# A final norm and the mixer behind it: the transposes taken from the unscaled X, with the reciprocal roots on a diagonal

## The reference, cut to what matters

```python
def rmsnorm(x, w):                       # first block's end: "final", gain final_norm
    return x * lax.rsqrt(jnp.mean(x * x, axis=-1, keepdims=True) + EPS) * w

x = first_block(...)                     # ... ffn, then rmsnorm(x, final_norm)
hn = _rms_norm(h, e_norm_mix[i])         # second block, layer 0: h = x
p = hn @ e_w_in[i]                       # input projection of the RWKV mixer
h = h + concat(ya, yb) @ e_w_out[i]      # the residual path needs the normed x itself
```

## Time and profile before

| | us |
|---|---|
| median of 3 runs | 1972.7 (1971.6 to 1972.93) |
| the profiled execution, whole | 1973.36 |
| its span in the profile | 1971.6 |
| PE busy in the span | 1919.0 (97%) |
| DVE busy | 1522.7 (77%) |
| ACT busy | 1149.5 (58%) |
| POOL busy | 374.2 (19%) |

### The profile page before, as it was taken

One profiled execution on the slowest core, in us unless ns is written; L12 is line 12 of the kernel. 1 busy time (PEld: TensorE's weight loads), 2 busy tenths in 40 slices (PEclk: granted clock), 3 DMA queues, 4 the chain that ended last, 5 costly groups with the idle time before them and its releaser, 6 DMA issues.

```text
span 1971.6 us, 33634 instructions
## 1 busy us (share of the span) xinstructions
PE 1919.0 (97%) x12652; PEld 1684.8 (85%) x12652; DVE 1522.7 (77%) x2142; ACT 1149.5 (58%) x1717; POOL 374.2 (19%) x181
## 2 busy tenths in 40 slices
PE   7999998999999999999999899999999999999998
PEld 6888997988888889988879888888997788888886
DVE  6777886777777778777767867777787699898987
ACT  5444565544454454654455555444566677777776
POOL 2222021322222220122222232322001100000000
PEclk9999999999999999999999999999999999999999
DMA  8655441555555554255553205655553599999995
GB/s 347 201 187 187 152 160 48 200 192 191 192 176 190 191 178 172 100 206 192 187 190 130 97 3 183 202 190 188 189 196 132 199 325 354 326 356 328 356 337 207
DMA packets 73689, 401.06 MB, mean 203 GB/s; under 512 B 8288, under 2 KB 8416, under 8 KB 41440
## 3 DMA queue, kind: packets, MB, share of 16 engines
q1 hardware_dynamic: 72992, 397.55, 58.1%
q10 hardware_dynamic: 576, 1.84, 0.3%
HBM read 398.30 MB, written 1.05 MB: 203 GB/s over the span
## 4 chain that ended last, share of the span: by engine, by line
PE 88%; DVE 6%; PEld 3%; ACT 2%; issue 1%; DMA 0%; SPq 0%; ACTq 0%; DVEq 0%; PEldq 0%
PE psum L823 20%; PE psum L345 14%; PE psum L346 14%; PE psum L347 14%; PE psum L803 11%; PE psum L578 2%; PE psum L590 2%; PE psum L580 2%; PE psum L1188 1%; PE psum L3753 1%; DVE w_lo L313 1%; PE psum L359 1%; PE psum L3766 1%; PE psum L436 1%; PEld psum L347 1%
## 5 line engine op out<-in xcount | busy, mean ns | idle before, releaser
L313 DVE TENSOR_TENSOR w_lo<-ring,w_hi 128x1024 fp32r<-128x1024 f32 x498 | 741.9, 1519 | 172.4 <-ACT w_hi L306 171.6
L306 ACT ACTIVATE w_hi<-ring 128x1024 fp32r<-128x1024 f32 x744 | 738.9, 1051 | 204.6 <-PEq L539 104.6
L319 POOL TENSOR_TENSOR w_lo<-ring,w_hi 128x1024 fp32r<-128x1024 f32 x132 | 325.5, 2466 | 1093.4 <-ACT w_hi L306 1093.4
L823 PE MATMUL psum<-fT,w_hi 128*128 128x512 f32 x1760 | 422.3, 391 | 3.8 <-ACT w_hi L306 3.8
L823 PEld LDWEIGHTS psum<-fT,w_hi 128*128 128x128 f32 x1760 | 330.5, 189 | 72.2 <-ACT w_hi L306 4.2
L803 PEld LDWEIGHTS psum<-fT,w_lo 128*128 128x128 f32 x1760 | 226.0, 191 | 8.9
L345 PE MATMUL psum<-w_hi,act_hi 128*128 128x512 f32 x594 | 232.9, 392 | 0.2 <-DVE act_lo L4091 0.2
L346 PE MATMUL psum<-w_lo,act_hi 128*128 128x512 f32 x594 | 232.5, 391 | 0.0
L347 PE MATMUL psum<-w_hi,act_lo 128*128 128x512 f32 x594 | 231.1, 389 | 0.0
L803 PE MATMUL psum<-fT,w_lo 128*128 128x256 f32 x1760 | 228.7, 283 | 0.0
L888 ACT ACTIVATE up_sums<-psum 128x512 f32<-128x512 f32 x110 | 65.7, 597 | 234.5 <-PE psum L803 234.5
(11 more groups left out here) (611 smaller groups left out, 2923.4 us busy)
## 6 DMA issues: line engine op xcount, KB each, us to landing
ring<-in_stream SPq DMA_DIRECT2D x249, 1024.0 KB, 5.6
ring<-in_stream SPq DMA_DIRECT2D x248, 512.0 KB, 4.3
tables<-in_tables SPq DMA_DIRECT2D x1, 2005.0 KB, 19.6
gain_row<-in_gains ACTq DMA_DIRECT2D x3, 512.0 KB, 5.2
rows<-in_rows SPq DMA_DIRECT2D x1, 1288.0 KB, 22.4
X<-in_x SPq DMA_DIRECT2D x1, 1024.0 KB, 4.9
columns<-in_columns SPq DMA_DIRECT2D x1, 993.0 KB, 15.4
result<-X SPq DMA_DIRECT2D x3, 256.0 KB, 2.9
```

The source lines that it names most:

```text
L306: act.activation(part(w_hi, g, i), ring[:, k, i * PART:(i + 1) * PART], ACT.Copy) \
L313: dve.tensor_tensor(part(w_lo, g, i), ring[:, k, i * PART:(i + 1) * PART], part(w_hi, g, i).bitcast(F32), ALU.subtract) \
L319: pool.tensor_tensor(part(w_lo, g, 2), ring[:, k, 2 * PART:STEP], part(w_hi, g, 2).bitcast(F32), ALU.subtract) \
L823: pe.matmul(psum[:, 4 + 2 * (s % 2) + o, :], w[0][:, o, k, :], fT[:, k, :, :].rearrange("p a c -> p (a c)"), start=k == 0, stop=False, ski ...
```

## The change

At the border between the final norm and the RWKV mixer the order is turned around. Let r0 be the reciprocal roots of the final norm.

- ACT squares X in halves of 512 features, each as soon as DVE has added it; the root of a token tile takes the second half's sum, with the first half's sum plus EPS as its bias. Sums, and the product of the two gains, lie in the still unused `rstd_row`.
- DVE makes the reciprocal roots and a diagonal matrix of them for each token tile.
- PE makes the transposes as ordinary products: a chunk of the unscaled X is the stationary operand, the diagonal the moving one, which gives the transposed and scaled chunk. Nine fillers stand ahead, not 16.
- ACT and DVE take the high and low halves with the product of both gains.
- X itself is scaled on DVE behind its low halves, by the same instruction as before.
- The splits of the second step's first two parts by ACT move from the FFN's end: one behind the roots, one behind the high halves.
- `final_gain` is a new part of the column table (eight numbers a partition), which moves what is allocated behind it by 32 bytes; `m_partial` of the last layer takes the place of an existing small tile.

```diff
@@ class Places
-                 (... ("conv3", 3 * 4)])
+                 (... ("conv3", 3 * 4), ("final_gain", KT)])
@@ network_kernel
+        half_squares = rstd_row[:, 0:2 * TT].rearrange("p (h t) -> p h t", h=2)
+        first_squares, both_gains = rstd_row[:, 2 * TT:3 * TT], rstd_row[:, 4 * TT:4 * TT + KT]
@@ head_scalar, head_vector: gain_of(n) becomes head_gain(n)
+        def head_gain(n):
+            return both_gains if from_final(n) else gain_of(n)
@@ ffn_scalar
-            split_hi(act, g0 + n + 1, g0 + n + 1, (0, 1))
+            if NETWORK[at + 1][0] != "final":
+                split_hi(act, g0 + n + 1, g0 + n + 1, (0, 1))
@@ new
+        def final_head_tensor(pe, n):
+            keep_warm(pe, psum[:, 7, :], 9)
+            for t, pairs in ((0, (0, 1)), (1, (0,)), (0, (2,)), (1, (1,)), (0, (3,)), (1, (2, 3))):
+                pe.wait_ge(*after(f"final {n} diag {t}"))
+                for p in pairs:
+                    for i in range(2):
+                        k = 2 * p + i
+                        ins = pe.matmul(head_bank(n, p)[:, (i * TT + t) * P:(i * TT + t + 1) * P], X[:, t, k * P:(k + 1) * P], rstd_diag[:, t, :],
+                                        start=True, stop=True, skip_group_check=True)
+                    if t == TT - 1:
+                        ins.then_inc(*norm.tensor(f"norm {n} turn {p}"))
+
+        def final_head_scalar(act, n):
+            load_gain_row(act, NETWORK[n - 1][1])
+            act.activation(warm[:, :], eps, ACT.Sqrt)
+
+            def square(h, t):
+                c = slice(h * 512, (h + 1) * 512)
+                act.wait_ge(*after(f"x {n - 1} {t} {4 * h}"))
+                act.activation(up_sums[:, h, :, :].rearrange("p o c -> p (o c)") if t == 0 else O[:, 1, c], X[:, t, c], ACT.Square, scale=D_MODEL ** -0.5,
+                               accum_out=half_squares[:, h, t:t + 1]).then_inc(*norm.scalar(f"final {n} square {h} {t}"))
+
+            def root(t):
+                act.wait_ge(*after(f"final {n} square 1 {t}"))
+                act.wait_ge(*after(f"final {n} first"))
+                act.activation(rms[:, t:t + 1], half_squares[:, 1, t:t + 1], ACT.Sqrt, bias=first_squares[:, t:t + 1]) \
+                   .then_inc(*norm.scalar(f"final {n} root {t}"))
+
+            square(0, 0)
+            square(0, 1)
+            square(1, 0)
+            root(0)
+            square(1, 1)
+            root(1)
+            g = first_step[n] + 1
+            split_hi(act, g, g, (0,))
+            head_scalar(act, n)
+            split_hi(act, g, g, (1,))
+
+        def final_head_vector(dve, n):
+            dve.wait_ge(*after(f"final {n} square 0 1"))
+            dve.tensor_tensor(first_squares[:, :], half_squares[:, 0, :], eps.to_broadcast([P, TT]), ALU.add).then_inc(*norm.vector(f"final {n} first"))
+            dve.tensor_tensor(both_gains[:, :], col("final_gain"), gain_of(n), ALU.mult).then_inc(*norm.vector())
+            for t in range(TT):
+                dve.wait_ge(*after(f"final {n} root {t}"))
+                dve.reciprocal(rstd[:, t:t + 1], rms[:, t:t + 1]).then_inc(*norm.vector())
+                dve.wait_ge(*norm.vector.so_far())
+                dve.tensor_scalar(rstd_diag[:, t, :], ident, rstd[:, t:t + 1], None, ALU.mult).then_inc(*norm.vector(f"final {n} diag {t}"))
+            head_vector(dve, n)
+            for t, ins in enumerate(gained(dve, n - 1, X)):
+                ins.then_inc(*norm.vector(f"x {n} {t}"))
@@ the last layer's tile
-            m_partial = take("m_partial", [P, TT])
+            m_partial = rstd_f
@@ the tensor program (scalar and vector programs likewise, and "final" itself only continues)
-                    keep_warm(pe, psum[:, 7, :], 16)
-                    head_tensor(pe, at)
+                    final_head_tensor(pe, at)
```

More of the change, by code:

```diff
@@ L74 @@
                  ("r_k", 4), ("sgu_b", 4), ("sgu_w", 4 * P), ("router", KT * EXPERTS), ("lora", 512), ("g2", 512),
-                 ("cmp_k2", 2 * 64), ("cmp_v2", 2 * 64), ("pos_k", 16), ("pos_v", 16), ("conv3", 3 * 4)])
+                 ("cmp_k2", 2 * 64), ("cmp_v2", 2 * 64), ("pos_k", 16), ("pos_v", 16), ("conv3", 3 * 4), ("final_gain", KT)])
 ROW = Places([("gdn_norm", P), ("diff_norm", P), ("ln_g", 512), ("ln_b", 512),
@@ L422, in operand, with from_final @@
             return (fT_hi, fT_lo) if NETWORK[n][0] == "ffn" else (hT_hi, hT_lo)
+        def from_final(n):
+            return n > 0 and NETWORK[n - 1][0] == "final"
+        def head_gain(n):
+            return both_gains if from_final(n) else gain_of(n)
         def head_bank(n, p):
@@ L443, in head_scalar @@
                     k = 2 * p + i
-                    act.activation(operand(n)[0][:, k, :], head_bank(n, p)[:, i * SEQ:(i + 1) * SEQ], ACT.Copy, scale=gain_of(n)[:, k:k + 1]) \
+                    act.activation(operand(n)[0][:, k, :], head_bank(n, p)[:, i * SEQ:(i + 1) * SEQ], ACT.Copy, scale=head_gain(n)[:, k:k + 1]) \
                        .then_inc(*norm.scalar(f"norm {n} hi {p}"))
@@ L452, in head_vector @@
                     k = 2 * p + i
-                    dve.scalar_tensor_tensor(lo[:, k, :], head_bank(n, p)[:, i * SEQ:(i + 1) * SEQ], gain_of(n)[:, k:k + 1], hi[:, k, :].bitcast(F32),
+                    dve.scalar_tensor_tensor(lo[:, k, :], head_bank(n, p)[:, i * SEQ:(i + 1) * SEQ], head_gain(n)[:, k:k + 1], hi[:, k, :].bitcast(F32),
                                              ALU.mult, ALU.subtract).then_inc(*norm.vector(f"norm {n} hT {k}"))
@@ L4196, in _ @@
                 if kind == "final":
[L4197 to L4201, removed]
+                    continue
+                if kind != "moe":
+                    if from_final(at):
+                        final_head_scalar(act, at)
+                    else:
+                        head_scalar(act, at, (3,) if after_mixer(at) else PAIRS)
                     if at == 0:
@@ L4219, in _ @@
                 if kind == "final":
-                    if NETWORK[at - 1][0] != "moe":
-                        final_vector(dve, at)
                     continue
                 if kind != "moe":
-                    head_vector(dve, at, (3,) if after_mixer(at) else PAIRS)
+                    if from_final(at):
+                        final_head_vector(dve, at)
+                    else:
+                        head_vector(dve, at, (3,) if after_mixer(at) else PAIRS)
                     if at == 0:
@@ L4397, in pack_columns @@
     c[:, COLUMN["gain"]] = np.concatenate([per(a[n].reshape(-1)) for n in names], axis=1)
+    c[:, COLUMN["final_gain"]] = per(a["final_norm"])
     c[:, COLUMN["conv"]] = np.concatenate([per(a["l0_conv_w"][j]) for j in range(4)], axis=1)
```

## The result

| | us |
|---|---|
| median, kernel before (22 runs beside these) | 1974.73 (1969.92 to 1978.52) |
| median, changed kernel (22 runs) | 1977.78 (1975.3 to 1985.46) |
| ratio | 1.002, 95% interval 1.0013 to 1.0026 |
| the profiled execution of the changed kernel, whole | 1981.05 |
| its span (before: 1971.6) | 1979.2 |

The forecast was 1969.2, and faster by 3.5; the kernel is slower by 0.2%, 3 us by the medians and some 4 by the ratio. (The forecast counted from a median of 3 runs, 1972.7. The 22 runs beside those of the changed kernel have 1974.73, from which the same 3.5 would give 1971.2.) One row of the table already says where to look: the change takes 7 fillers out (7 x 0.226 = 1.6) and gives products of 3.88 for transposes of 3.29, which is 1 us less work, and yet PE is busy 10 us longer. So most of the time isn't in a wait.

What follows compares the result with a forecast made beforehand. PE was taken as the bound (88% of the span), so only its waits at the border could be won: the last low half from 1041.6 to 1038.1 saves 3.5, all else zero; 1972.7 - 3.5 = 1969.2, range 1967.9 to 1971.0.

Steps and rivals of the forecast that it cites:

- The border's terms: Border of final norm and RWKV: the steps from ACT's table load to the last low half at about 1038.1, saving 3.5.
- The sum of the first halves: DVE adds EPS to the first halves' sum at the border: 0.16 taken; with 0.95 all that follows is 0.8 later.
- the rival of four times a transpose: At the border each product with a 32-bit diagonal takes 0.43, 16 of them 6.9; time 1971.2, chance 0.04.
- the first rival: At the border the product costs four times a transpose: last turn 1038.9, T 1040.1, time 1971.2; chance 0.04.
- T: End of the last low half at the border: 1041.60 before, forecast about 1038.1.
- the second: The clock falls at the border all the same: 16 products take 7.2, T 1040.8, time 1971.9; chance 0.03.
- What moved behind the head: DVE's scaling of X and work behind the last low halves come later but stay hidden, with cover 0.8 and 0.6.
- The rival that made this the bound: PE waits for row product or third part behind the border: 0.5 to 1.5 lost, time 1969.9 to 1970.9; chance 0.07.
- slower than before: PE's holes in RWKV fall to half clock, at most 1.7 each; three cost 5.1, time 1974.3; chance 0.02.
- more than I count: Last layer's half-clock stretch of 6.8 shortens, up to 1.7; products 0.4 more; time 1967.5 to 1968.7; chance 0.30.

## Why the prediction was wrong, and where it was right

**The step that failed** is the one that reads "Nothing lies outside the border but the 32-byte move of the tiles behind the column table. No row shows its cost; I take zero, with half a microsecond to either side". It costs 5.6 us of PE's time by the lags, 5.9 by the starts; by the ratios of the changed kernel and of the one with the distance restored, 1.002 and 0.9986, it is 6.7 with an uncertainty of some 2.5, and by the comparison at one clock below it is 6.0 with 0.9. It acts on every product that reads hT, and so in four mixers. The half microsecond was no bound at all: no row had been put under it. The only bound that the rows could give was the number of products times a change of pitch, and in the kernel before the starts of otherwise equal products lie 113 ns apart in some runs of them and 117 to 118 in others. With those 5 ns for every one of the 2090, the bound would have been 10 us to the slow side, and the range would have held the result.

**The border's terms** held, each read from line 951's start, with the forecast's own distance from 1028.17 behind it: table load -0.72 (-0.73), first square 0.79 (0.79), root 0 at 2.96 (2.98), first product 3.83 (3.86), first high half 5.51 (5.53), first low half 6.38 (6.43), projection 7.47 (7.48), last low half 9.82 (9.93). The sum of the first halves, with bounds 0.16 and 0.95, took 0.15: the value taken from the nearer row was right, and the 0.95 was that of an instruction beside POOL's; no run here puts the same instruction with and without POOL side by side. The product with a 32-bit diagonal took two records at full clock: the eight of the first diagonal in the whole-tile version last 1.16, and 32 with all waits 3.88; so the rival of four times a transpose falls (16 x 0.43 would be 6.9). That a transpose takes half as long as such a product at full clock, an estimate in the prediction, is borne out: in the kernel with the move alone the clock fell only at 1039.8, and the transposes start 0.11 apart until then and 0.21 apart behind it, against 0.226 for a product.

Two slips in the rivals' sums changed nothing. Five falls of the clock at 1.7 would give 1977.7, not 1977. And the first rival puts T 1.2 behind its last turn, the second 1.6, with products of nearly the same length.

**What moved behind the head** stayed under cover. The diagonal of the next norm was ready at 1046.40 + 0.48 = 1046.88, 5.87 behind the last low half (6.0 forecast), and PE wanted it at 1047.99. POOL's low half ended 8.92 behind it (9.1 forecast):

```profile
1047.54 2.39 POOL L321 TENSOR_TENSOR w_lo<-ring,w_hi 128x1024 fp32r<-128x1024 f32 x1 [14.60 <-ACT w_hi L308]
```

PE had no wait there. The rival that made this the bound didn't come true.

**The clock.** The rival "slower than before" needed three falls of the clock in RWKV's holes to end slower, at 1.7 each. In the profiled execution there is one, longer than I had allowed for, at 2.9. So the kernel did come out slower, but not by that rival's mechanism. Nor need the stretch be the border's doing: the kernel before with all tiles moved, whose border and products' pace are as before, has it too, from 1152.2 to 1162.5:

```profile
1152.00:1162.00 10.00, 9.58 (x170) 8.99 (x171) 2.99 (x7) 5.24 (x13) 2.62 (x3) 0.51 0.01 2
```

Of the ten kernels with the products at the border, five show a stretch of 10 us there and five one of 3.4 or none; of the three with the old border, one does. The half-clock stretch at the last layer, on which the rival "more than I count" rested, was 6.8 long before and in the changed kernel, 3.4 in the version without the move and absent with the distance restored. These stretches are one execution's, and a single profile says nothing on what a kernel does to them.

Every execution has its mean granted clock on record, though, and that says more. Within a kernel an execution is 1.24 us longer (1.13 to 1.35) for each 0.001 by which its mean clock is lower. (That is a fit with one slope for all kernels. It leaves out two executions of the kernel before, with mean clocks of 0.751 and 0.947; all others lie at 0.989 to 0.998.) Read off this line at a mean clock of 0.995, the kernels stand so:

| kernel | us at a mean clock of 0.995 |
|---|---|
| change without the move | 1970.4 |
| change, distance restored | 1970.5 |
| 16 fillers; whole-tile squares | 1971.9; 1971.9 |
| no fillers (its low clock is in part its own doing) | 1971.4 |
| before, beside three groups of runs | 1973.1, 1973.1, 1972.6 |
| before, all moved | 1972.8 |
| 128, 32, 64 nearer | 1974.0, 1975.0, 1975.4 |
| changed kernel, moved by 64 | 1976.5, 1976.4 |
| the move alone | 1978.6 |

The price of the lost distance is then 1976.5 - 1970.5 = 6.0 (0.9 to either side) with the new border and 1978.6 - 1972.8 = 5.9 (1.3) with the old one, as the 5.6 and 5.9 from the traces say. The three nearer distances cost 3.7, 4.7 and 5.0 (1.0 to 1.3 to either side), so the 1.0035 of the 64 nearer is in good part the clock of its five executions, 0.992 in the mean. The mean clocks of the changed kernel and of the kernel before are alike, 0.994 each, so nothing points to the shorter border as a cause of more half clock.

**What stays open.** RWKV's small products from 1110 to 1148 lag by 2.3 in the changed kernel. The two other kernels with the old border lag there by 0.6 and 1.5, the ten with the new one by 0.8 to 3.3, at whatever distance of the tiles. Much of it is idle time of PE: 1.6 more than before in the changed kernel and with the distance restored, 0.5 and 0.9 more in the two with the old border. It may be that some 1 us of the border's gain is given back there, by a chain that doesn't run through the projection. At one clock the best version is 2.2 to 2.7 ahead of the kernel before (0.9 to either side), where D gained 3.1 to 3.6. That fits, but the uncertainty doesn't exclude that nothing is given back.

On the hardware side, the Trainium skill ("SBUF — State Buffer", section "SBUF: two separate sides") says that among the engines PE never waits on anyone, contention being confined to the port pair that two other engines share. The trace agrees with it in so far as the products lose their 3 ns with the other engines idle too (173.2 against 176.8). The runs also show that PE's own pace depends on where hT and w lie to each other, which that rule gives no reason to expect; where in the chip the 3 ns arise, no run here shows.

## What to carry to other kernels

A change of a few bytes in a table moves every tile allocated behind it, and where PE bounds the kernel that can have a price of its own: compare the addresses of the matrix operands before and after, and hold their distance with a small tile put elsewhere, before anything is concluded about the change itself. An edit for which no row shows a cost isn't thereby free; multiply the instructions that it touches by the spread among equal ones, and put that in the range. When two versions differ by a few tenths of a per cent, compare them at one mean clock, if the clock of every execution is known. And run the suspected side effect alone: one kernel with nothing but the padding told more than the whole profile of the change.

## What the runs showed that I had not expected

- Where hT lies in SBUF relative to the tiles of w changes the pace of the products of the two: 115.3 to 115.7 ns from start to start at 61504 bytes against 117.2 to 119.9 at the five other distances, for hT_hi by w_lo. At 32 bytes more that is 0.3% of the kernel's time.
- It is the place relative to each other that matters: with both moved by 32 bytes the pace is as before.
- Within a hole of 2.25 us on PE, with work on both sides, the clock fell to half for 3.4 us; with holes of 0.39 and 0.21, and with none (nine fillers), it stayed at full. Behind the old border's holes, 1.7 and 0.9, it fell 7.8 us behind the first addition to X in one profile, 8.8 and 8.9 in two others.
- Transposes of 32-bit data start 0.11 us apart at full clock and 0.21 at half.
